# A first norm by quarters of the width, on turned tokens, in a two-block transformer kernel

## The reference, cut to what matters

```
mod = silu(c) @ w_ada + b_ada                 # c is one row of 1024; w_ada is 1024 x 6144
sh1, sc1, g1, sh2, sc2, g2 = split(mod, 6)
h = rms_norm(x, norm1_g) * (1 + sc1) + sh1    # 256 x 1024
mix = token_mixer(h, w_in, rel_bias, ...)     # h @ w_in first: retention heads, then 12 attention heads
x = x + g1 * mix                              # then the second norm, an MLP, and the whole second block
```

## Time and profile before

| | us |
|---|---|
| median of three runs | 1362.06 |
| the profiled execution | 1361.76 |
| its span, first to last instruction | 1360.0 |
| PE busy | 1304.6 (96%) |
| DVE busy | 888.4 (65%) |
| ACT busy | 736.3 (54%) |
| POOL busy | 641.2 (47%) |

### The profile page before, as it was taken

One profiled execution on the slowest core, in us unless ns is written; L12 is line 12 of the kernel. 1 busy time (PEld: TensorE's weight loads), 2 busy tenths in 40 slices (PEclk: granted clock), 3 DMA queues, 4 the chain that ended last, 5 costly groups with the idle time before them and its releaser, 6 DMA issues.

```text
span 1360.0 us, 18658 instructions
## 1 busy us (share of the span) xinstructions
PE 1304.6 (96%) x6684; PEld 1083.6 (80%) x6684; DVE 888.4 (65%) x1383; ACT 736.3 (54%) x1107; POOL 641.2 (47%) x512
## 2 busy tenths in 40 slices
PE   7999999999999999999999999999989999899997
PEld 4778788899887788888787887888868787788885
DVE  6783884354444564214678667888867867788777
ACT  5343454344464444445566437666745663667664
POOL 3898899988868699998400420000060034000000
PEclk9999999999999999999999999999999999999999
DMA  9868468746544455555531018878854300688782
GB/s 373 318 261 309 155 246 318 247 156 248 191 150 170 169 186 186 186 188 184 215 126 63 1 51 314 311 282 326 292 189 168 104 22 1 232 309 299 285 311 94
DMA packets 45496, 280.03 MB, mean 206 GB/s; under 512 B 5565, under 2 KB 8893, under 8 KB 13918
## 3 DMA queue, kind: packets, MB, share of 16 engines
q1 hardware_dynamic: 38434, 263.82, 53.5%
q10 hardware_dynamic: 6974, 15.05, 3.1%
HBM read 274.66 MB, written 4.19 MB: 205 GB/s over the span
## 4 chain that ended last, share of the span: by engine, by line
PE 73%; DVE 12%; POOL 5%; DVEq 4%; ACT 3%; issue 2%; DMA 1%; ACTq 1%; SPq 0%; POOLq 0%
PE AC L1315 9%; PE AC L1317 9%; PE AC L1316 9%; PE G L1315 8%; PE G L1317 8%; PE G L1316 8%; POOL w_lo L721 5%; PE T L1507 2%; PE G L1507 2%; DVE w_lo L2195 2%; PE G L1353 1%; PE G L1352 1%; PE G L1351 1%; PE T L1508 1%; PE G L1508 1%
## 5 line engine op out<-in xcount | busy, mean ns | idle before, releaser
L721 POOL TENSOR_TENSOR w_lo<-w_raw,w_hi 128x512 fp32r<-128x512 f32 (+1 forms) x470 | 611.6, 1337 | 322.3 <-ACT w_hi L784 311.2
L784 ACT ACTIVATE w_hi<-w_raw 128x1024 fp32r<-128x1024 f32 x444 | 467.3, 1059 | 391.2 <-PE AC L1317 165.4
L2195 DVE TENSOR_TENSOR w_lo<-w_raw,w_hi 128x1024 fp32r<-128x1024 f32 x228 | 275.6, 1223 | 52.7 <-ACT w_hi L784 44.4
L1315 PE MATMUL AC<-w_hi,yT_hi 128*128 128x512 f32 x368 | 145.3, 395 | 0.9 <-POOL w_lo L721 0.9
L1317 PE MATMUL AC<-w_hi,yT_lo 128*128 128x512 f32 x368 | 142.7, 388 | 0.0
L1316 PE MATMUL AC<-w_lo,yT_hi 128*128 128x512 f32 x368 | 142.6, 387 | 0.0
L1315 PE MATMUL G<-w_hi,arena_r 128*128 128x512 f32 x320 | 128.2, 401 | 4.4 <-DVE w_lo L3065 2.3
L1317 PE MATMUL G<-w_hi,arena_r 128*128 128x512 f32 x320 | 125.1, 391 | 0.0
L1316 PE MATMUL G<-w_lo,arena_r 128*128 128x512 f32 x320 | 124.8, 390 | 0.0
L1315 PE MATMUL G<-w_hi,xT 128*128 128x512 f32 (+1 forms) x240 | 98.4, 410 | 5.6 <-DVE xT L2347 2.1
L1315 PE MATMUL AC<-w_hi,xT 128*128 128x512 f32 x240 | 97.5, 406 | 3.3 <-POOL w_lo L721 2.3
(11 more groups left out here) (514 smaller groups left out, 2537.5 us busy)
## 6 DMA issues: line engine op xcount, KB each, us to landing
w_raw<-w_stream SPq DMA_DIRECT2D x148, 1024.0 KB, 5.1
w_raw<-w_expert SPq DMA_DIRECT2D x94, 1024.0 KB, 5.2
arena<-w_stream SPq DMA_DIRECT2D x8, 512.0 KB, 12.1
mod<-rows ACTq DMA_DIRECT2D x2, 2048.0 KB, 9.1
rel_scratch<-arena ACTq DMA_DIRECT2D x1, 3072.0 KB, 12.7
w_raw<-w_expert SPq DMA_DIRECT2D x4, 512.0 KB, 4.4
mod<-rows ACTq DMA_DIRECT2D x3, 476.0 KB, 3.9
x_sb<-x SPq DMA_DIRECT2D x1, 1024.0 KB, 8.3
```

What stands on the lines that cost most here:

```text
L721: i = pool.tensor_tensor(w_lo[:, k % SLOTS, cols], w_raw[:, raw, cols], w_hi[:, k % SLOTS, cols].bitcast(F32), ALU.subtract)
L784: act.activation(w_hi[:, k % SLOTS, :], w_raw[:, raw, :], ACT.Copy).then_inc(hi_ready, 1)
L1315: pe.matmul(out, xh, wh, start=start, stop=False)
L2195: dve.tensor_tensor(w_lo[:, k % SLOTS, :], w_raw[:, k % RAW, :], w_hi[:, k % SLOTS, :].bitcast(F32), ALU.subtract).then_inc(lo_ready, 1)
```

## The change

- **Quarters.** Shift and scale come in four quarters of 256 columns (`ada_quarter`). A chunk is now 128 x 512; the sum over chunks is held in a PSUM bank (`sum_bank`) except at its two ends. In quarter 0 PE multiplies the last chunk itself. `w_ada`'s first part is laid out in memory by quarters; quarter q is two transfers of 1024 KB. Quarter 0 goes to `w_raw` slots 4 to 7, the others to `arena`.
- **Turned tokens.** ACT scales x by the inverse root alone (two 128x1024), PE turns the result by chunks of 128 columns (`quarter_turn`, 4 transposes), and four matmuls of one column each sum shift and scale over the partitions, one number per partition (`quarter_sums`). DVE then applies gain, scale and shift as numbers per partition straight from PSUM (`turned_quarter`: two small adds and products, two 128x256 products, two 128x256 subtractions), with ACT rounding in between. The full rows of the gain, of the bias and the clearing of `mod` go.
- **Order of units.** Quarter u lets PE run unit u of tiles 0, 1 and 2: three units per quarter. After the first it turns the next quarter, before the third it sums it.
- **Bias rows** are made by 3 matmul pairs with 4 rows each instead of 12 with 128, copied out by 3 ACT copies, stored as 12 rows of 2 KB, and spread in memory by three copies from memory to memory (4 heads x 128 rows of 2 KB each), which ACT issues in its rounds j = 7, 9 and 11. The wait before the next stage is for 64 (all four).
- **Loads.** SP issues x and the identity first, then quarter 0, units 0 and 1, quarter 1, and so on; the pieces of `w_ada` from the second on come later (`ADA_AFTER`), and DVE's calls of them move: pieces 0 and 1 behind `rotate(2)` and `rotate(3)`, 2 behind tile 4, 3 to where 4 was, and 4 into `group_norm(0)`. `DVE_LO` begins with units 10 and 11 instead of 0 and 8.

```diff
+ADA_AFTER = {18: 1, 22: 2, 26: 3, 30: 4, 34: 5, 40: 6, 46: 7, 52: 8, ..., 90: 15}
+DVE_LO = [U_RET_IN + 10, U_RET_IN + 11] + [U_RET_IN + UP * j - 1 for j in (11, 12, 13)]
...
+            sp.dma_start(sm[:, 336:336 + 4 * KC], A["c_col"]).then_inc(c_loaded, 16)
+            sp.dma_start(x_sb[:, :, :], A["x"]...).then_inc(x_loaded, 16)
+            sp.dma_start(ident[:, :], A["identity"]).then_inc(ident_loaded, 16)
+            piece(0, 2)
+            piece(1, 3)
+            first_units(0)
+            quarter(1)
+            first_units(1)
+            sp.wait_ge(ada_used, KC // 2)
+            piece(2 * n_ring + 2, 2)
+            quarter(2)
+            lows_done(PIECE)
+            piece(3 * n_ring, 0)
+            sp.wait_ge(ada_used, 2 * KC)
+            quarter(3)
+            lows_done(2 * PIECE)
+            piece(3 * n_ring + 1, 1)
...
 # ACT
+            act.wait_ge(rstd_done, 1)
+            for t in range(TOK):
+                act.activation(xs[:, t, :], x_sb[:, t, :], ACT.Copy, scale=var[t]).then_inc(h_ready, HALVES)
+            his(U_RET_IN, U_RET_IN + 2)
+            turned_quarter(0)
+            for g in range(len(GROUPS)):
+                act.wait_ge(bias_row, g + 1)
+                act.activation(bias_vec[:, g, :], row_banks[g], ACT.Copy).then_inc(bias_rows_out, 1)
+            his(U_RET_IN + 2, U_RET_IN + PRE + 2)
+            for q in range(1, QUARTERS):
+                turned_quarter(q)
+                his(U_RET_IN + PRE * q + 2, U_RET_IN + min(PRE * (q + 1) + 2, PRE * UP - 1))
...
+                if j in (7, 9, 11):
+                    g = (j - 7) // 2
+                    heads = slice(g * AH, (g + 1) * AH)
+                    act.wait_ge(bias_stored, 16)
+                    act.dma_start(A["rel_scratch"][heads, 0:P, :], A["rel_scratch"][heads, P:P + 1, :].to_broadcast([AH, P, NT])).then_inc(bias_stored, 16)
...
-            act.wait_ge(bias_stored, 16)
+            act.wait_ge(bias_stored, 64)
 # PE
+            def quarter_sums(q):
+                pe.wait_ge(ada_summed, q + 1)
+                for i in range(2 * QC):
+                    o = pe.matmul(sum_cols(q)[:, i:i + 1], mod1[:, q, i * P:(i + 1) * P], ones_col, start=True, stop=True)
+                o.then_inc(scale_sum, 1)
...
+            pe.wait_ge(h_ready, HALVES * TOK)
+            quarter_turn(0)
+            quarter_sums(0)
+            keep_busy(G[:, 0, :], 8)
...
+            for u in range(QUARTERS):
                 for j in range(PRE):
+                    k = first_unit(j, u)
+                    if j == PRE - 1 and u + 1 < QUARTERS:
+                        quarter_sums(u + 1)
+                    low_half(0, k)
...
+                    if j == 0 and u + 1 < QUARTERS:
+                        quarter_turn(u + 1)
 # DVE
+            rstd(0, sm[:, 16:18], 1.0 / D, 1e-6, lambda: ada_quarter(0, 0, 1))
+            ada_quarter(0, 1, PE_SUM)
...
+            turned_quarter(0)
+            ada_quarter(1, 0, KC)
+            ada_quarter(2, 0, 1)
+            turned_quarter(1)
+            ada_quarter(2, 1, KC)
+            ada_quarter(3, 0, 1)
+            turned_quarter(2)
+            ada_quarter(3, 1, KC)
+            turned_quarter(3)
+            dve_lo(0)
             dve_lo(1)
...
+                if h == 0:
+                    ada_piece(4)          # inside group_norm(0), ahead of the gain
...
-            ada_piece(0)
             rotate(0)
-            ada_piece(1)
             rotate(1)
             rotate(2)
+            ada_piece(0)
+            rotate(3)
+            ada_piece(1)
+            ret_in_tile(4)
             ada_piece(2)
-            rotate(3)
-            ada_piece(3)
-            ret_in_tile(4)
             ret_in_tile(5)
...
             decayed(1)
-            ada_piece(4)
+            ada_piece(3)
```

More of the change, by code:

```diff
@@ L80 @@
 U_MIX = 16 * 6
[L81 to L84, removed]
+QUARTERS = 4
+QC = KC // QUARTERS
+QW = 2 * QC * P
+ADA_FIRST = QUARTERS * KC
+N_SUMMED = QUARTERS - 2
+PE_SUM = KC - 1
+ADA_AFTER = {18: 1, 22: 2, 26: 3, 30: 4, 34: 5, 40: 6, 46: 7, 52: 8, 56: 9, 60: 10, 66: 11, 72: 12, 78: 13, 84: 14, 90: 15}
+DVE_LO = [U_RET_IN + 10, U_RET_IN + 11] + [U_RET_IN + UP * j - 1 for j in (11, 12, 13)]
 U_JOINED = U_ATT_FIRST + UP
@@ L608, in _ @@
             n_ring = RAW // PIECE
[L609 to L617, removed]
@@ L618, in _ @@
-            sp.dma_start(ident[:, :], A["identity"]).then_inc(ident_loaded, 16)
[L620 to L640, removed]
+            sp.dma_start(sm[:, 336:336 + 4 * KC], A["c_col"]).then_inc(c_loaded, 16)
+            sp.dma_start(x_sb[:, :, :], A["x"].rearrange("b (t p) d -> p (b t) d", p=P)).then_inc(x_loaded, 16)
@@ new lines, in _, with first_units, quarter @@
+            sp.dma_start(ident[:, :], A["identity"]).then_inc(ident_loaded, 16)
+            piece(0, 2)
+            piece(1, 3)
+            def first_units(s):
+                for u in range(PIECE):
+                    sp.dma_start(w_raw[:, s * PIECE + u, :], A["w_stream"][2 * n_ring + s][:, u * UNIT:(u + 1) * UNIT]).then_inc(raw_landed[s], 16)
+            def quarter(q):
+                for h in range(2):
+                    sp.dma_start(quarter_home[2 * q + h], A["w_stream"][2 * q + h]).then_inc(quarter_landed[2 * (q % 2) + h], 16)
@@ L645, in _, with ada_piece @@
             sp.dma_start(pos_i[:, :], A["pos_col"]).then_inc(pos_loaded, 16)
+            def ada_piece(i):
+                sp.wait_ge(ada_used, ADA_FIRST + PIECE * i)
+                piece((i + 2) * n_ring + n_ring - 1, n_ring - 1)
             for r in range(1, U_MIX // (RAW - PIECE)):
[L647 to L651, removed]
+                for s in range(2 if r == 1 else 0, n_ring - 1):
+                    n = (RAW - PIECE) * (r - 1) + PIECE * (s + 1)
+                    lows_done(n)
                     piece((r + 2) * n_ring + s, s)
+                    if n in ADA_AFTER:
+                        ada_piece(ADA_AFTER[n])
                 if r == 2:
@@ new lines, in _, with turned_quarter @@
+            dve.memset(sm[:, 892:893], 0.0).then_inc(rstd_done, 1)
+            ada_quarter(0, 1, PE_SUM)
+            dve.wait_ge(scale_sum, 1)
+            dve.tensor_tensor(b_col[:, 0:2 * QC], G[:, 1, 0:2 * QC], b_col[:, 0:2 * QC], ALU.add).then_inc(ada_used, 1)
+            dep()
+            def turned_quarter(q):
+                cols, b = slice(QC * q, QC * (q + 1)), b_col[:, 2 * QC * q:2 * QC * (q + 1)]
+                dve.wait_ge(scale_sum, q + 2)
+                dve.tensor_tensor(b, sum_cols(q), b, ALU.add)
@@ L2335, in first_normed @@
                 dep()
-                for t in range(TOK):
-                    scaled(t, c, W[:, 0:D], h_sb[:, t, half(c)])
+                dve.tensor_tensor(a_col[:, cols], b[:, QC:2 * QC], g_col[:, cols], ALU.mult)
                 dep()
-                dve.wait_ge(mod_out, c + 1)
-                for t in range(TOK):
-                    dve.tensor_tensor(h_sb[:, t, half(c)], h_sb[:, t, half(c)], mod1[:, c, 0, :], ALU.add).then_inc(h_ready, 1)
-                if c == 0:
-                    dve_lo(0)
@@ new lines, in turned_quarter @@
+                dep()
+                for i in range(QC):
+                    c = QC * q + i
+                    dve.wait_ge(chunk_hi, c + 1)
+                    dve.tensor_tensor(xT_lo[:, c, :], h_full[:, i * S:(i + 1) * S], xT_hi[:, c, :].bitcast(F32), ALU.subtract).then_inc(chunk_lo, 1)
+            turned_quarter(0)
[5 more added lines that the diff above has]
+            turned_quarter(2)
```

218 lines of the change are left out of this document (93 added, 125 removed).

## The result

The changed kernel takes 1368.07 us, the median of 8 runs (1366.24 to 1372.26), where the kernel before took 1362.32 (8 runs, 1359.82 to 1364.44) beside it. The ratio is 1.0048, with a 95% interval of 1.0038 to 1.0058. The forecast was 1353 with a range of 1348 to 1360: wrong in its sign, and the time is outside the range. What came true is rival 4, the last copy that holds ACT, to which 0.09 was given. The profiled execution took 1368.85, its span is 1367.1, 7.1 more than before's.

What follows compares the result with a forecast made beforehand. PE, busy 96% of the span, was taken to bound the kernel. From 1361.76 us, -11.4 by unit 20 and +2.9 for the w_ada pieces, with the copies free, gave 1353.3, said as 1353; range 1348 to 1360.

Steps and rivals of the forecast that it cites:

- rival 4: Before the turned y: the last copy holds ACT, deciding from about 19 us of copy time; 1366 to 1368 us, chance 0.09.
- The copies: Three 1 MB copies within memory before the turned y: 8.4 us each, bounds 4.2 and 25, 10 us free, cost 0.
- Unit 0: Start of the kernel: PE starts unit 0 at 19.2 us, 9.2 earlier than before.
- Quarters on PE: Units 0 to 11: PE hardly waits for the quarters, DVE and POOL keep up, unit 11 ends at 59.0 us.
- the ramp of 1.7: PE's quarters: a stretch at half clock costs 1.7 us, bounds 0 and 3.4.
- Rotations: Ahead of unit 12: they set its start at 63.1 us, gain 9.2; unit 20 at 88.3, gain 11.4.
- the slack of 3 us: Before unit 12: PE is ready at 60.1 us, so 3 us of the gain is lost waiting for the rotations.
- Pieces of w_ada: Piece 4 in the first group norm adds 4.3 us to DVE; 2.9 reaches unit 47, bounds 0 and 4.3.
- Bias rows at the start: Old matmuls, copies and 3 MB store lay beside other work except through units 12 and 13, counted in the rotations.
- The sum: Whole kernel: -11.4 at unit 20 and +2.9 for the pieces give -8.5 us, 1353.3 from 1361.76.
- Rival 1: First group norm to unit 47: DVE absorbs piece 4, so its 2.9 us cost vanishes; 1350 us, chance 0.20.

Runs made afterwards that it cites:

- e2: The changed kernel with its three copies written with the 128 rows outermost instead of the 4 heads: 1357.69 us, 0.9965 of the kernel before.
- e8: The changed kernel with one 3 MB copy in round 9, 12 heads outermost, instead of three copies: 1354.18 us, 0.9942 of the kernel before.
- e1: The changed kernel with the same three copies one round earlier (j = 6, 8, 10): 1359.63 us, 0.9982 of the kernel before.
- e3: e2 with piece 4 of w_ada inside the group norm cut to 32 of 1024 columns, load kept: 1354.87 us, 0.9942 of the kernel before.
- e9: e5 with its three spread copies in rounds 6, 8, 10 instead of 7, 9, 11: 1354.46 us, 0.9933 of the kernel before.
- e7: The kernel before with only the bias part of the change, copies with rows outermost in rounds 7, 9, 11: 1366.13 us, 1.0031.
- e10: e7 with its copies in rounds 6, 8, 10: 1362.14 us, 1.0001 of the kernel before.
- e5: e2 with piece 4 behind piece 3, pieces 2 to 6 loaded earlier, gain and offset rows issued in round 3: 1351.63 us, 0.9929.

## Why the prediction was wrong, step by step

- **The copies: the step that failed.** The prediction's "Lower bound 4.2 each [...], upper 25; I take 8.4, twice the store's, as both ends are memory" and "So 10 us are free: cost 0". Measured 20.40 us for the last, ACT held for 10.80, PE for 9.64, and then about 2.4 more at half clock (lag 3.5 at the end of the late transposes, 5.4 five microseconds on). The copy went out at 186.61, as forecast (194.2 less 8.5), and the slack was 9.7, close to the 10 taken. Rival 4 had the mechanism: it had the wait decide from 19 us of copy time on. That its 1366 to 1368 meets the time is in part luck: 1368 stood for a copy of 25 us, and for one of 20.4 its sum gives 1353.3 + 10.4 = 1363.7. The other 5.2 us of the profiled execution are 0.7 less gain at unit 20, 1.2 more for the pieces, 1.6 more at the copy (12.0 with the half clock, for 10.4), and 1.7 behind it, none of them in the rival. What failed was the choice between the bounds. It reasoned by bytes and row size, from a store with 128 partitions outermost; the copy's 4 outermost was in the diff and was not read as the number of engines at work. Nor was it asked what the loads, on the same engines, leave to such a copy: a fifth of its rate. e2 and e8 show that the outermost dimension is the cause. With the copy in either form, the kernel is 10 to 14 us faster than the changed one.
- **Unit 0** was forecast at 19.2 and came at 21.40. DVE's chunks ended at 16.0 where 15.4 was taken, and the sums began at 16.24; their eight records of one column took 1.86, where 1.05 was taken (and is met in the next quarters), and the chain behind them, from 18.14 to 21.40, took 3.3 for 2.3 to 2.6. DVE's timeline shows the first small operation on two SBUF inputs at 1.28 us and its like in the next quarter at 0.57, both with POOL at work, and one on a PSUM and an SBUF input at 0.16:

```profile
18.14 0.16 DVE L2354 TENSOR_TENSOR sm<-T,sm 128x4 f32<-128x4 f32 x1 [1.85 <-PE T L1552]
18.38 1.28 DVE L2356 TENSOR_TENSOR sm<-sm 128x2 f32<-128x2 f32 x1
...
29.54 0.57 DVE L2356 TENSOR_TENSOR sm<-sm 128x2 f32<-128x2 f32 x1
```

- **Quarters on PE** held: PE waits twice 0.46 us in them and no more, and the ramp of 1.7 did not come in this execution. In e1, e2, e3 and e9 the clock was at half for 6.8 us from about 15 us on, and unit 0 came at 21.3 to 21.5 all the same: at this place the stretch costs next to nothing.
- **Rotations** held: unit 12 at 63.1, measured 63.89, its releaser the DVE rotation; unit 20 at 88.3, measured 88.97. Gain there 10.7 for 11.4. That 2.2 us lost at unit 0 are 0.8 at unit 12 is due to the slack of 3 us that PE had ahead of the rotations: `rotate(0)` began at 55.11 for 54.5, after 1.01 us of waiting for PE's tile.
- **Pieces of w_ada.** "Cost 2.9" was about the right size by e3 (2.8, with the reserve said there). In the changed kernel's own profile the lead falls by 4.1 from unit 20 to unit 47, near the upper bound of 4.3. The place was half right: PE waits 2.32 at unit 43 already, and 1.91 at unit 47.
- **Bias rows at the start**: "lay beside other work except through units 12 and 13". The exception is a wrong reading: in e7 the 3 MB store is gone and unit 12 starts at 72.19, as before. So the store did not make units 12 and 13 late, and e10 shows that the whole part is worth nothing by itself in the kernel before, 1.0001. The sum did not suffer, as it took unit 12 from the rotations.
- **The sum**: -10.7 + 4.1 + 12.0 (from a lead of 6.6 to a lag of 5.4) + 1.7 = +7.1. Without the copies' 12.0 it would be -4.9; e2, which is that kernel, is 4.8 under the kernel before in its median. So close a match is partly luck: e2's own profiled execution, at a clock of 0.990, is only 2.8 shorter in its span.
- **The 1.7 behind the turned y** was no term of the prediction. The changed kernel's clock has a half-clock stretch of 3.4 us at 810 that before's has not (both have one more, near 1005 and 1012). Across it the lag, read from the same matmuls in both traces, grows from 5.6 at 807 to 6.95 at 818. Why one more of these stretches falls into some executions is open.
- **A smaller slip.** Rival 1 has contended operations "swing by a factor of two (0.69 to 1.78)"; that is a factor of 2.6. Its price, 2.9, does not hang on it.

## What to carry to other kernels

Read the outermost dimension of a transfer's pattern before its bytes: in these runs it set how many DMA engines worked on a copy, and with 4 outermost 1 MB took 20.4 us against about 7 with 128. Ask also what the loads leave to such a copy while both run. A transfer whose price no row shows, with a wait behind it that covers the critical engine, deserves a chance that follows its bounds (here 4.2 to 25 us, with the decision at 19), and not the comfort of the middle value. And a faster copy is no free copy: on all engines it pushed back the load issued behind it (to 205.4 us in e7), so move it to where no load is urgent.

## What the runs showed of the hardware

- A copy within memory of 1 MB in rows of 2 KB took 20.40 us with 4 outermost, about 7 us with 128 outermost, and 3 MB took about 17 us with 12 outermost. Alone in flight, the first ran at a share of 0.26 and 100 GB/s, the last at 0.79 and 307 (e8, 166 to 168 us).
- Beside loads that use all engines, the copy with 4 outermost fell from 100 to about 20 GB/s (the changed kernel, 196 to 200 us: 0.08 MB in 4 us).
- A wait of PE can be dearer than its length: after 9.64 us of waiting here the clock was still 0.50 for 5 us of work, about 2.4 us more; after 2.71 us in e7, 3.4 us at half clock. It does not always follow: behind the wait of 2.3 us at unit 43 the clock fell to half for 3.4 us in e2 and stayed at 1.00 in the changed kernel. A part of the scatter within one kernel (e5: 1349.43 to 1355.87) goes with the clock: the mean granted clock of e5's six runs is 0.999 at 1349.43 and 0.991 at 1355.87.
- With its bias rows nearly gone, PE in e7 stood 7.68 us before the first sums, and its clock fell to 0.50 in that wait.
